# Attention of a two-layer hybrid block: value product in plain fp32, queries split ahead of the units, unit loop written out

## The reference

```python
q, k, v = diff_qkv(pc, q_norm_g[l], k_norm_g[l])         # 4 heads, 2 branches of 64, values of 128
k_all = jnp.concatenate([k, kc], axis=1)                 # 1280 keys
s = jnp.einsum('bqhcd,bkhcd->bhcqk', q, k) * (QK_DIM ** -0.5)
p = jax.nn.softmax(s, axis=-1)
a = p[:, :, 0] - lam * p[:, :, 1]
o = jnp.einsum('bhqk,bkhe->bqhe', a, v)
```

## Time and profile before

| | us |
|---|---|
| median of three runs | 4933.3 |
| span of the profiled execution, first to last instruction | 4915.3 |
| TensorE busy (19082 matmul records) | 3974.9 |
| DVE busy | 2237.0 |
| ScalarE busy | 1142.1 |
| attention units of layer 0, window | 299.7 |
| keys and queries of layer 0, window | 54.8 |

### The profile page before, as it was taken

How to read it: one execution, slowest core, us unless ns; L and a number is a source line. 1 busy time by engine, 2 the same in 40 slices (tenths; PEclk the granted TensorE clock), 3 DMA queues, 4 the chain that set the end, 5 groups by cost and what they waited for, 6 DMA issues and landing times. The chain is left out here.

```text
span 4915.3 us, 48809 instructions
## 1 busy us (share of the span) xinstructions
PE 3974.9 (81%) x19082; PEld 3242.4 (66%) x19082; DVE 2237.0 (46%) x2941; ACT 1142.1 (23%) x1714; POOL 115.6 (2%) x140
## 2 busy tenths in 40 slices
PE   7898877652885879999999798767628857999998
PEld 6786654541774758888888586535527745888886
DVE  1304426243885145444544503444348833455555
ACT  1311110012554042221111411110125523222221
POOL 0000000100000000000000000100000000000000
PEclk9888866885996889999999898868869978999999
DMA  5331220104001201111110342121040030111111
GB/s 182 101 109 63 73 99 32 62 35 117 0 1 60 99 28 44 34 39 38 38 39 20 120 137 64 48 73 71 30 107 1 0 111 26 56 46 52 46 50 52
DMA packets 278520, 295.42 MB, mean 60 GB/s; under 512 B 9376, under 2 KB 247968, under 8 KB 276770
## 3 DMA queue, kind: packets, MB, share of 16 engines
q1 hardware_dynamic: 269924, 256.91, 16.5%
q0 software_dynamic: 8448, 36.44, 2.4%
HBM read 242.19 MB, written 51.12 MB: 60 GB/s over the span
## 5 line engine op out<-in xcount | busy, mean ns | idle before, releaser
L435 PE MATMUL banks<-gh,uhi 128*128 128x512 f32 (+1 forms) x1760 | 652.3, 371 | 41.9 <-DVE gl L407 41.9
L436 PE MATMUL banks<-gh,ulo 128*128 128x512 f32 (+1 forms) x1760 | 651.6, 370 | 0.0
L437 PE MATMUL banks<-gl,uhi 128*128 128x512 f32 (+1 forms) x1760 | 650.8, 370 | 0.0
L937 DVE SCALAR_TENSOR_TENSOR xT<-banks,mod,xT 128x512 f32<-128x512 f32 (+1 forms) x440 | 303.4, 698 | 705.6 <-PE banks L437 705.6
L435 PE MATMUL banks<-hh,whi 128*128 128x512 f32 (+1 forms) x944 | 388.9, 412 | 47.3 <-DVE hl L407 30.9
L435 PEld LDWEIGHTS banks<-gh,uhi 128*128 128x128 f32 x1760 | 334.3, 190 | 100.3 <-issue 33.8
L437 PEld LDWEIGHTS banks<-gl,uhi 128*128 128x128 f32 x1760 | 334.0, 190 | 56.2
L436 PEld LDWEIGHTS banks<-gh,ulo 128*128 128x128 f32 x1760 | 334.3, 190 | 55.6
L436 PE MATMUL banks<-hh,wlo 128*128 128x512 f32 (+1 forms) x944 | 366.0, 388 | 0.0
L437 PE MATMUL banks<-hl,whi 128*128 128x512 f32 (+1 forms) x944 | 363.5, 385 | 0.0
L435 PE MATMUL banks<-fhi,dhi 128*128 128x512 f32 (+1 forms) x880 | 330.5, 376 | 24.3 <-DVE dlo L929 15.8
(11 more groups left out here) (244 smaller groups left out, 6749.8 us busy)
## 6 DMA issues: line engine op xcount, KB each, us to landing
uraw<-in_ffn_w_up SPq DMA_DIRECT2D x88, 512.0 KB, 4.1
wmodpair<-in_w_mod SPq DMA_DIRECT2D x40, 1024.0 KB, 5.3
wraw<-in_w_in SPq DMA_DIRECT2D x44, 512.0 KB, 6.2
draw<-in_ffn_w_down SPq DMA_DIRECT2D x176, 128.0 KB, 3.9
p_mid<-stage POOLq DMA_DIRECT2D x30, 640.0 KB, 3.5
fw<-in_fwd SPq DMA_DIRECT2D x4, 2816.0 KB, 9.6
x_mid<-xT SPq DMA_DIRECT2D x2, 5120.0 KB, 20.2
kraw<-p_mid SPq DMA_DIRECT2D x32, 320.0 KB, 8.3
```

The lines of the kernel that those rows point to most:

```text
L435: pe.matmul(out, wh, xh, start=first, stop=False)
L436: pe.matmul(out, wl, xh, start=False, stop=False)
L437: return pe.matmul(out, wh, xl, start=False, stop=last)
L937: dve.scalar_tensor_tensor(xT[:, o, t0:t0 + w], dacc[(o * NCH + c) % 2][:, 0:w], k.mod[:, 40 + o, a:a + 1], xT[:, o, t0:t0 + w], ALU.mult, ...
```

## The change

In `k_phase` the queries go the way of the keys: SP loads them tile by tile through the same two buffers, behind the keys; ScalarE makes the high part, already times 0.125, and DVE the low part in the lower 64 rows of `qstack`, which now holds all units. GpSimd's two transfers are gone. `v_phase` keeps the turned values once, as plain fp32 (`vt`). In `attend_phase` there is no staging in a unit; the maximum is negated in the reduction itself; the exponential has no scale; the turned probabilities are copied once as plain fp32 (`probs_turned`, by ScalarE alone); the value product is one plain fp32 matmul a block. The units are written out without a hardware loop, in another order.

The diff, cut to its core:

```diff
 k_phase
-            for m in range(8):
+            for m in range(16):
                 if m >= 2:
                     sp.wait_ge(s_lo.sem, s_lo.at(m - 1))
+                w = T if m < 8 else W
                 for half in range(2):
-                    r = K0 * P + 64 * m
-                    sp.dma_start(raw[64 * half:64 * half + 64, m % 2, :], k.dram["p_mid"][r:r + 64, :]
+                    r = (K0 if m < 8 else Q0) * P + 64 * (m % 8)
+                    sp.dma_start(raw[64 * half:64 * half + 64, m % 2, 0:w], k.dram["p_mid"][r:r + 64, 0:w]
                                  ).then_inc(s_in[m % 2].sem, 16)
-        @block.gpsimd
-        def _(pool):
-            for half in range(2):
-                pool.dma_start(q2[64 * half:64 * half + 64, :, 0:W],
...
+                    act.activation(qs[:, m - 8, 0:W], raw[:, m % 2, 0:W], ACT.Copy, scale=0.125).then_inc(s_hi.sem, 1)
...
+                    low = qs[64:P, m - 8, 0:W]
+                    dve.scalar_tensor_tensor(low, raw[64:P, m % 2, 0:W], 0.125, low.bitcast(F32), ALU.mult, ALU.subtract
+                                             ).then_inc(s_lo.sem, 1)
 v_phase
-        @block.vector
-        def _(dve):
-            for h in range(HEADS):
-                dve.wait_ge(s_hi.sem, s_hi.at(h + 1))
-                dve.tensor_tensor(vl[:, :, h * P:(h + 1) * P],
...
 attend_phase, TensorE
+            def values(n):
+                h = n // nq
+                if n >= 1:
+                    pe.wait_ge(s_ok.sem, s_ok.at(n))
+                for j, blocks in enumerate(groups):
+                    pe.wait_ge(s_ke.sem, s_ke.at(n * NGR + min(max(j, 1) + 1, NGR)))
+                    for b in blocks:
+                        last = pe.matmul(O, at[:, b, :], vt[:, k0 // P + b, h * P:(h + 1) * P], start=b == 0,
+                                         stop=b == NKB - 1)
+                last.then_inc(s_pv.sem, 1)
+            for n in range(NU):
+                if n + 1 < NU:
+                    scores(n + 1, 1)
+                for j in range(NGR)[:2]:
+                    turn(n, j)
+                if n + 2 < NU:
+                    scores(n + 2, 0)
+                if NGR > 2:
+                    turn(n, 2)
+                values(n)
 attend_phase, ScalarE
+            def exp(n, c):
+                act.wait_ge(s_nm.sem, s_nm.at(n * 2 + c + 1))
+                if n >= 1:
+                    act.wait_ge(s_cb.sem, s_cb.at(n))
+                act.activation(e[:, c, 0:NK], S[c], ACT.Exp, bias=mx[:, c:c + 1], accum_out=den[:, n, c:c + 1]
+            for n in range(NU):
+                if n + 1 < NU:
+                    exp(n + 1, 0)
+                for j in range(NGR)[:2]:
+                    keep(n, j)
+                if n + 1 < NU:
+                    exp(n + 1, 1)
+                if NGR > 2:
+                    keep(n, 2)
+                if n >= 1:
+                    square(n - 1)
 attend_phase, DVE
+            def maximum(n, c):
                 dve.wait_ge(s_sc.sem, s_sc.at(n * 2 + c + 1))
-                dve.reduce_max(mx[:, c:c + 1], S[c], AX.X).then_inc(s_mx.sem, 1)
-                dve.wait_ge(s_mx.sem, s_mx.at(n * 2 + c + 1))
-                dve.tensor_scalar(mx[:, c:c + 1], mx[:, c:c + 1], -0.125, None, ALU.mult).then_inc(s_nm.sem, 1)
+                dve.reduce_max(mx[:, c:c + 1], S[c], AX.X, negate=True).then_inc(s_nm.sem, 1)
+            for n in range(NU):
+                if n + 1 < NU:
+                    maximum(n + 1, 0)
+                combine(n)
+                if n >= 1:
+                    keep(n - 1)
+                if n + 1 < NU:
+                    maximum(n + 1, 1)
```

More of the change, by code:

```diff
@@ L1731, in attend_phase @@
         O = ps[:, 3584:3712]
[L1733 to L1757, removed]
+        @block.tensor
+        def _(pe):
+            def scores(n, c):
+                h, i = n // nq, n % nq
+                if n >= 1:
+                    pe.wait_ge(s_ex.sem, s_ex.at(n * 2 + c - 1))
+                q = qs[:, 2 * h + c, q0 + i * P:q0 + (i + 1) * P]
+                for t0, w in cuts:
+                    for kx in (kh, kl):
+                        last = pe.matmul(S[c][:, t0:t0 + w], q, kx[:, 2 * h + c, k0 + t0:k0 + t0 + w],
+                                         start=kx is kh, stop=kx is kl)
+                last.then_inc(s_sc.sem, 1)
+            def turn(n, j):
+                if j == 0:
+                    pe.wait_ge(s_cb.sem, s_cb.at(n + 1))
+                    if n >= 1:
+                        pe.wait_ge(s_ke.sem, s_ke.at(n * NGR))
+                elif j == 1 and n >= 1:
+                    pe.wait_ge(s_ok.sem, s_ok.at(n))
+                elif j == 2:
+                    pe.wait_ge(s_ke.sem, s_ke.at(n * NGR + 1))
+                for x, b in enumerate(groups[j]):
+                    last = pe.transpose(TR[j % 2][:, x * P:(x + 1) * P], am[:, b * P:(b + 1) * P], k.ident)
+                last.then_inc(s_tr.sem, 1)
+            def values(n):
+                h = n // nq
+                if n >= 1:
+                    pe.wait_ge(s_ok.sem, s_ok.at(n))
+                for j, blocks in enumerate(groups):
[4 more added lines that the diff above has]
+                last.then_inc(s_pv.sem, 1)
+            scores(0, 0)
+            scores(0, 1)
+            if NU > 1:
+                scores(1, 0)
+            for n in range(NU):
[8 more added lines that the diff above has]
+                values(n)
@@ L1759, in _ @@
         @block.scalar
         def _(act):
[L1761 to L1766, removed]
+            def exp(n, c):
[3 more added lines that the diff above has]
+                act.activation(e[:, c, 0:NK], S[c], ACT.Exp, bias=mx[:, c:c + 1], accum_out=den[:, n, c:c + 1]
+                               ).then_inc(s_ex.sem, 1)
@@ L1782, in round_ @@
[L1782 to L1798, removed]
-                    act.activation(junk[:, :], oraw[:, bass.ds(n - 2, 1), :].rearrange("p a c -> p (a c)"), ACT.Square,
-                                   accum_out=ss[:, bass.ds(n - 2, 1)]).then_inc(s_osq.sem, 1)
@@ L1807, in _ @@
+            exp(0, 0)
+            exp(0, 1)
+            for n in range(NU):
[7 more added lines that the diff above has]
+                    keep(n, 2)
+                if n >= 1:
+                    square(n - 1)
+            square(NU - 1)
         @block.vector
         def _(dve):
[L1809 to L1812 removed]
```

198 lines of the change are left out of this document (60 added, 138 removed).

## The result

The changed kernel takes **4770.05 us** (median of four, 4767.23 to 4777.89) against 4934.84 us for the kernel before (four, 4929.19 to 4945.56): ratio 0.9677, 95% interval 0.9653 to 0.9701, 3.2% faster. The forecast was 4795 us in a range of 4755 to 4885. So sign and range held, and the fall was 165 us where 138 were forecast.

| term | predicted, us | measured in the traces, us |
|---|---|---|
| units and end, layer 0 | -78 | -83.3 (300.0 to 216.7) |
| units and end, layer 1 | -78 | -87.6 (302.9 to 215.3) |
| 256-key phase | -7 | -11.1 (37.15 to 26.09) |
| keys and queries, both layers | +28 | +27.2 (13.7 and 13.4) |
| values, both layers | -3 | -2.7 |

A forecast was written before the change was run, and what follows sets the result against it. The prediction took a loop of waits to set the unit, with TensorE and vector engine nearly full. Terms -156 (units and ends), -7, +28, -3 sum to -138; 4915.3 - 138 + 18.0 = 4795 us, range 4755 to 4885.

The forecast's parts named there:

- units and end, layer 0: Layer 0's 32 attention units: 72 us less over 31 steps (8.88 to 6.56 us each), 6 less at the end.
- 256-key phase: Layer 0's eight units over 256 keys, some 33 us: 7 us less, between 0 and 12.
- The loop of waits: Chain of waits across engines from one attention unit's C to the next: 6.56 us a unit, where 8.88 stood.
- C: The mix of the two softmax rows on the vector engine in each attention unit, taken at 1.55 us.
- TensorE as the second limit right behind: TensorE's own work in an attention unit: 5.8 us, some 0.7 us to spare.
- Value product: Ten plain fp32 products a unit, 0.22 us a block by the gating step's rows: 2.2 us, 1.1 less than before.
- the rival at 0.44: Plain fp32 as four full passes, 0.44 us a block: TensorE sets units at 8.0 us, 4884 us total; chance 0.10.
- The negated maximum: Negation inside the unit's maximum over 1280 columns: taken at 1.49 us, with 0 and 0.16 more as ends.
- End of a phase: Last C to last square in an attention phase: 9 us for 14.8, between 7 (full clock) and 11 (half).
- Keys and queries: Loading stretch with one queue and two tiles: 68.0 us in layer 0, 64.5 in layer 1, together +28 us.
- The rival "loading free": Key and query loading set by bandwidth alone, so 0 us is added there: 4767 us; chance 0.07.
- Clock falls: Rival: TensorE's clock falls in attention and stays down, about 11 us a unit, 5089 us; chance 0.05.

## Why the prediction was right, point by point

- **The loop of waits.** Right, link by link: predicted 1.60 (C to exponential), 1.55 (to the scores), 1.46 (to the maximum), 1.50 (to the small steps) and 0.45 (to C), in sum 6.56; measured 1.65, 1.47, 1.46, 1.41 and 0.45, in sum 6.44. The 0.12 too much is the exponential's link, a straight unit's 1.55 where 1.47 was measured, and a maximum counted at its length of 1.50 though its successor starts 1.41 after it; 0.05 too little from C to the exponential hides a part of both. It also puts C to C just below the 6.5 to 6.6 that the prediction named as its sign. Over 62 steps that is 7 of the 15 us by which the units gained more than forecast. Another 3 are layer 1, whose steps before took 8.98 in the mean (3677.26 to 3955.61), and I had used layer 0's 8.88 for both. The two kernels with more on TensorE and the one with a link less show that this loop, and not TensorE, sets the unit.
- **TensorE as the second limit right behind.** Right, a little pessimistic: 5.8 against 5.65, room 0.8 where 0.7 was forecast.
- **Value product.** 0.22 a block from the gating rows, measured 0.22; the rival at 0.44 is refuted. The Trainium skill, page "FP8 and Floating Point Precision", section "TensorE Precision Notes", has true FP32 at four passes. What fails is to read these as four passes at the 0.11 of a 128-column one. At full clock the kernel before has reduced passes of 512 columns 0.23 us apart, those of 256 columns 0.11 to 0.12 and those of 128 columns 0.11 (the rows below, and the earlier trace rows): a reduced pass of 128 columns is hardly cheaper than one of 256. A plain product takes two records at every width: 0.43 each at 512 columns (two gating records start at 1129.84 and 1130.27 us), 0.216 at 256 and 0.112 at 128. So at 512 columns it costs 0.86, close to four reduced passes as the page says; at 128 columns it costs two. Three reduced passes are 0.69 at 512 columns, some 0.35 at 256 and 0.33 at 128; of these widths the plain product (0.86, 0.43, 0.22) is cheaper at 128 columns alone.

```profile
3742.01 0.39 PE L1867 MATMUL banks<-klo,qstack 128*128 128x512 f32 x1
3742.24 0.28 PE L1867 MATMUL banks<-khi,qstack 128*128 128x256 f32 x1
3742.35 0.28 PE L1867 MATMUL banks<-klo,qstack 128*128 128x256 f32 x1
```

What the saved 1.1 us of TensorE are worth depends on the order. The prediction prices it for the new order alone: at 0.33 a block 6.9 us a unit in place of 6.56 (its 4818 us for that is 4816 by its own terms). By the measured 5.65 it would be some 6.75 against the loop's 6.44, about 0.3 us a unit, an estimate and not run. In the old order, which the prediction did not look at, they were worth nothing while the low halves stayed.

- **The negated maximum.** Taken at 1.49, measured 1.49. What it saves is on the loop, 0.19 us a unit.
- **End of a phase.** Predicted 9 us from the last C to the last square; measured 1437.62 to 1444.34, 6.7, the end that was given for full clock, since the last passes ran at 1.00 now. Both layers together save 16 us there in place of 12. That, a start of layer 1 that is 1.1 us shorter and the short last steps, less the two longer first ones, are the rest of the 15. The half clock that the prediction read from 1500 to 1505 us lies in the middle of that end and is not its last five microseconds; the clock had fallen at 1497.4 us, 1 us behind a pause of TensorE of 1.67 us.
- **The 256-key phase.** Mis-sized: -11.1 for -7. Its unit fell from 4.08 to 2.82 us, by more than the large ones did in proportion. I had taken less off for TensorE at half clock; it did run at 0.50, without a pause, from 1462.80 to 1475.64 us, with 2.82 us a unit, but the clock then rose and the last two steps took 2.52 and 2.36.
- **Keys and queries.** Right in mechanism and size: 68.3 us (68.0 forecast), and 62.7 (64.5) in layer 1, where the query tiles' rounds took 6.7 to 7.5 us, 7.0 in the mean, not 7.2. That the two tiles are the cause is shown by the four tiles. The rival "loading free" is refuted for two tiles, and its 0 was no lower bound either: with four tiles the stretch is 3.1 and 4.9 us shorter than before the change.
- **Clock falls.** Did not happen: 1.00 from 1243.5 us on, with one pause of 0.52 us a unit. The kernel with the new order and the splits had falls, though other ones than the rival's, which stay down: they came and went in most units, at a price of 1.2 us each. So the rival could not be ruled out from the share of idle time alone.
- **Left open:** the medians fell by 7 us more than the traced stages (164.8 and 157.5), and the stages that the change does not touch differ by 11 us the other way. Executions differ in them by up to 20 us, and no run was made to follow it.

## What to carry to other kernels

Follow one unit from a marker instruction to the next through every engine that it waits for, with start-to-start times from the timeline, and write TensorE's own work beside it: both numbers together told what most of the later edits were worth to 0.1 us a unit. The three largest misses are 0.25 to 0.4: TensorE's own work, put at 5.9 from its visible pause and measured at 5.65 (twice), and the new order with splits, 9.3 against 8.92 at full clock. Price an edit in the order in which it will run: freeing an engine that only waits gives nothing, and an order that suits one set of steps (no low halves) can lose with another. The plain fp32 product paid here at 128 columns; at 256 or 512 columns the same rows give the split as the cheaper one on TensorE. Where work moves out of a unit into a loading phase, give that phase enough tiles to keep the transfers going; two were short by a third, four filled it.

## What the runs showed of the hardware that was not expected

- In the kernel with the new order and splits TensorE's clock fell and rose again in most units, with 7.49 us busy in a full-clock unit of 8.92 and one pause of 1.20 us. It stayed at 1.00 in the straight unit of the kernel before that the earlier trace rows come from, busy 7.49 of 8.57 us with a pause of 1.07 us. Each fall lasted three to four us. Nothing here shows which of the differences decides.
- One queue with 32 transfers and four tiles moved keys and queries faster (51.5 us from the first transfer, share 0.95) than the two queues of the kernel before with two tiles (54.6 us, share 0.87). Tiles and queues changed together, so their parts are not told apart; with two tiles the one queue was slower (68.3 us, share 0.65).
- A plain fp32 product of 128 columns takes two records 0.112 us apart, the spacing that one reduced fp32 pass has at this width too (0.11). At 128 columns the plain product is thus two thirds of the price of the three-pass split; at 512 columns it is a quarter dearer (0.86 against 0.69).
- The negation inside a maximum over 1280 columns cost nothing (1.49 us with and without it); as an instruction of its own it cost 0.19 us on the loop.
